# Two layers of a streaming encoder on one core: expert weights in wider pieces, the first expert's rows picked in two fp32r parts, tiles moved in SBUF, empty slots not gathered

## What is computed

```python
def moe_ffn(x, w_r, wg, wu, wd):
    xt = x.reshape(-1, D)
    logits = jnp.dot(xt, w_r, preferred_element_type=F32)
    top_v, top_i = lax.top_k(logits, TOP_K)
    w = jax.nn.softmax(top_v, axis=-1)
    gates = jnp.einsum('tk,tke->te', w, jax.nn.one_hot(top_i, N_EXPERTS, dtype=F32))
    y = jnp.zeros(xt.shape, F32)
    for e in range(N_EXPERTS):
        h = jax.nn.silu(xt @ wg[e]) * (xt @ wu[e])
        y = y + gates[:, e:e + 1] * jnp.dot(h, wd[e], preferred_element_type=F32)
    return y.astype(x.dtype).reshape(B, L, D)
```

## Time and profile before

| | us |
|---|---|
| median of 3 runs | 1627.2 (1627.18 to 1627.65) |
| profiled execution, own time | 1622.71 |
| its span, first to last instruction | 1620.9 |
| TensorE busy in the span | 1566.9 (97%) |
| VectorE / ScalarE / GpSimd busy | 1236.4 / 1000.6 / 224.7 |
| mean granted TensorE clock | 0.985 |

### The profile page before, as it was taken

The page is one execution under the profiler, slowest core; times in us unless marked ns, Lnnn a source line. Parts: engine busy times, 40 slices in busy tenths (PEclk is TensorE's granted clock), DMA queues, the critical chain, the costliest instruction groups (busy, mean ns, idle before and its releaser), DMA issues.

```text
span 1620.9 us, 21665 instructions
## 1 busy us (share of the span) xinstructions
PE 1566.9 (97%) x8425; PEld 1346.0 (83%) x8425; DVE 1236.4 (76%) x1243; ACT 1000.6 (62%) x1077; POOL 224.7 (14%) x271
## 2 busy tenths in 40 slices
PE   7989999999998999999999999999999999999996
PEld 5978899999997887888888888888888888888885
DVE  4866666664476655988888888888888888888884
ACT  4554533333455445777777777777777777777774
POOL 4703220000150223202002002002002002002000
PEclk8999999999999997999999999999999999999998
DMA  6432554444433257999999999999999999999992
GB/s 176 131 102 81 106 167 142 141 161 143 137 114 113 92 111 274 347 385 361 384 371 359 381 370 355 386 378 357 383 372 359 382 371 354 387 373 353 388 359 79
DMA packets 222517, 437.03 MB, mean 270 GB/s; under 512 B 11829, under 2 KB 65921, under 8 KB 222417
## 3 DMA queue, kind: packets, MB, share of 16 engines
q1 hardware_dynamic: 214196, 420.40, 73.6%
q0 software_dynamic: 5968, 11.84, 2.7%
q10 hardware_dynamic: 2252, 3.41, 0.7%
HBM read 428.04 MB, written 13.34 MB: 272 GB/s over the span
## 4 chain that ended last, share of the span: by engine, by line
PE 86%; DVE 6%; ACT 4%; DMA 2%; issue 1%; POOL 1%; ACTq 0%; POOLq 0%; DVEq 0%
PE bank L1856 25%; PE bank L2305 13%; PE bank L2304 13%; PE bank L2309 13%; PE bank L2318 6%; PE bank L2324 6%; PE bank L2315 6%; DVE cut_lo L1250 2%; ACT cut_hi L855 2%; PE bank L2333 2%; PE bank L1859 1%; DMA ring<-ffn_w_up 1%; ACT pe L954 1%; DMA ring<-w_in 1%; POOL acc L654 1%
## 5 line engine op out<-in xcount | busy, mean ns | idle before, releaser
L1686 DVE TENSOR_TENSOR split_lo<-raw,split_hi 128x2048 fp32r<-128x2048 f32 x336 | 768.1, 2290 | 120.0 <-ACT split_hi L1121 119.4
L1121 ACT CAST split_hi<-raw 128x2048 fp32r<-128x2048 f32 x336 | 640.1, 1909 | 245.7 <-PE bank L2309 158.5
L2304 PE MATMUL bank<-split_hi,xgT_hi 128*128 128x512 f32 x896 | 357.3, 399 | 0.0
L2305 PE MATMUL bank<-split_hi,xgT_lo 128*128 128x512 f32 x896 | 355.8, 397 | 0.0
L1250 DVE TENSOR_TENSOR cut_lo<-ring,cut_hi 128x1024 fp32r<-128x1024 f32 x124 | 154.3, 1245 | 138.8 <-ACT cut_hi L855 138.6
L1856 PE MATMUL bank<-xT_hi,cut_hi 128*128 128x320 f32 x752 | 241.5, 321 | 5.0 <-DVE xT_lo L1264 2.3
L2309 PE MATMUL bank<-split_lo,xgT_hi 128*128 128x512 f32 x896 | 245.1, 395 | 0.0
L855 ACT CAST cut_hi<-ring 128x1024 fp32r<-128x1024 f32 x124 | 129.6, 1048 | 176.8 <-PE bank L1856 170.8
L1856 PE MATMUL bank<-xT_lo,cut_hi 128*128 128x320 f32 x752 | 235.8, 314 | 0.0
L1856 PE MATMUL bank<-xT_hi,cut_lo 128*128 128x320 f32 x752 | 234.4, 312 | 0.0
L2309 PEld LDWEIGHTS bank<-split_lo,xgT_hi 128*128 128x128 f32 x896 | 168.3, 188 | 41.0
(11 more groups left out here) (283 smaller groups left out, 1615.4 us busy)
## 6 DMA issues: line engine op xcount, KB each, us to landing
raw<-moe_w_gate SPq DMA_DIRECT2D x112, 1024.0 KB, 8.2
raw<-moe_w_up SPq DMA_DIRECT2D x112, 1024.0 KB, 8.2
raw<-moe_w_down SPq DMA_DIRECT2D x112, 1024.0 KB, 6.3
ring<-w_in SPq DMA_DIRECT2D x15, 1024.0 KB, 5.5
ring<-ffn_w_gate SPq DMA_DIRECT2D x11, 1024.0 KB, 5.6
ring<-ffn_w_up SPq DMA_DIRECT2D x11, 1024.0 KB, 5.3
ring<-ffn_w_down SPq DMA_DIRECT2D x10, 1024.0 KB, 5.1
ring<-w_out SPq DMA_DIRECT2D x8, 1024.0 KB, 5.0
```

What stands on the lines that cost most here:

```text
L1121: return nc.scalar.copy(split_hi[:, i % SR, :], raw_piece(i)).then_inc(hi_ready, 1)
L1686: V.tensor_tensor(split_lo[:, i % SR, :], raw_piece(i), split_hi[:, i % SR, :].bitcast(F32), ALU.subtract).then_inc(lo_ready, 1)
L2304: TE.matmul(o, xgT_hi[:, kk, :], hi[:, c], start=kk == 0, stop=False)
L2305: TE.matmul(o, xgT_lo[:, kk, :], hi[:, c], start=False, stop=False)
```

## The change

It does the following.
- Pieces: column tiles are taken in pairs. A gate (or up) piece holds 256 rows of two neighbouring tiles (1024 columns), four gate pieces and then four up pieces per pair; the seventh tile stays as it was. In a piece, each stationary operand is used for both tiles before the next. Silu and the products of a pair are made together.
- w_down's rows are assigned to partitions so that four neighbouring rows lie in one partition; to match, the transposes of hm take every fourth column.
- The first expert's rows: x gets a high part xr_hi (a second copy by ScalarE from PSUM) and a low part xr_lo (GpSimd, six subtractions), and the pick multiplies both with Gown in fp32r.
- Gathers skip slots without a token (index out of bounds), so xg is set to zero once.
- Tiles: `empty` is gone, Gown lies behind hs, two paddings (below_xg, below_hmT_lo) are added. By the allocation order, front and loop tiles up to split_lo move 384 bytes down, xg, xgT and hs 1728 bytes down, hmT_lo 1344 bytes up. x, raw and the constants stay.
- The square of the rows goes to hs instead of xhat, one copy is moved ahead of it, and the wait for k_out ahead of four copies.

```diff
-HT_AT = [4 * _j + 11 for _j in range(FC - 1)] + [4 * FC + 7]
+WIDE = FC // 2
+GROUPS = [(8 * _g, 4, (2 * _g, 2 * _g + 1)) for _g in range(WIDE)] + [(8 * WIDE, 2, (FC - 1,))]
+HT_AT = [_a + 2 * _n + 5 + _i for _a, _n, _ms in GROUPS[:-1] for _i in range(2)] + [4 * FC + 7]
+SILU_AT = {_a + _n - 1 + SR: (_a + _n, _ms) for _a, _n, _ms in GROUPS}
+GATED_AT = {_a + 2 * _n - 1 + SR: (_a + 2 * _n, _ms) for _a, _n, _ms in GROUPS}
+
+def gate_up(q):
+    a, n, ms = GROUPS[min(q // 8, WIDE)]
+    up, s = divmod(q - a, n)
+    return up, s, ms
...
-        empty = sb("empty", [P, MAXB * NE * 4])
...
+        xr_hi = sb("xr_hi", [P, NT, D], FR, token_rows)
...
-        Gown = sb("Gown", [P, NT, P])
...
+        sb("below_xg", [P, 48])
         xg = sb("xg", [P, D])
...
         hs = sb("hs", [P, 2, 512])
+        Gown = sb("Gown", [P, NT, P], FR)
+        sb("below_hmT_lo", [P, 384])
+        token_rows = ExitStack()
+        xr_lo = sb("xr_lo", [P, NT, D], FR, token_rows)
...
-            wd_v = A["moe_w_down"][0].rearrange("e (c b p) n -> e c p b n", b=4, p=P)
+            wd_v = A["moe_w_down"][0].rearrange("e (c p b) n -> e c p b n", b=4, p=P)
...
-                        w = wg_v if j % 2 == 0 else wu_v
-                        src = w[bass.ds(e + h, 1), :, 4 * half:4 * half + 4, 512 * (j // 2):512 * (j // 2) + 512]
+                        up, s, ms = gate_up(q)
+                        n = 4 // len(ms)
+                        src = (wu_v if up else wg_v)[bass.ds(e + h, 1), :, n * s:n * s + n, 512 * ms[0]:512 * (ms[-1] + 1)]
...
-            pool.dma_start(table.rearrange("(p n) c -> p (n c)", p=P), empty[:]).then_inc(table_zero, 16)
+            pool.dma_start(table.rearrange("(p n) c -> p (n c)", p=P), A["const"][:, CONST_W:CONST_W + MAXB * NE * 4]).then_inc(table_zero, 16)
...
+            R, job = norm_end(3, KB - 1)
+            pool.wait_ge(R.full, R.filled(job))
+            for half in range(2):
+                c = slice(512 * half, 512 * half + 512)
+                for t, (t0, rows) in enumerate(TILES):
+                    R = (RS, RC)[half]
+                    pool.wait_ge(R.free, R.emptied(("xk", t, half)))
+                    nc.gpsimd.tensor_tensor(xr_lo[0:rows, t, c], x[0:rows, t, c], xr_hi[0:rows, t, c].bitcast(F32), ALU.subtract).then_inc(xr_lo_ready, 1)
+            nc.gpsimd.memset(xg[:], 0.0).then_inc(pool_zero, 1)
             for t, (t0, rows) in enumerate(TILES):
                 pool.wait_ge(rows_sq, t + 1)
                 rsqrt(rs_slot(1, "end", t), rows, D, 1)
...
+                pool.indirect_dma_start(out=xg[:], out_offset=None, in_=hx[:, :], in_offset=bass.IndirectOffsetOnAxis(ap=idc[:, 0:1], axis=0),
+                                        bounds_check=T - 1, oob_is_err=False).then_inc(xg_in, 16)
...
-                nc.scalar.copy(x[0:rows, t, 512 * half:512 * half + 512], R.bank(("xk", t, half))[0:rows, :]).then_inc(R.free, 1)
+                c = slice(512 * half, 512 * half + 512)
+                nc.scalar.copy(x[0:rows, t, c], R.bank(("xk", t, half))[0:rows, :])
+                nc.scalar.copy(xr_hi[0:rows, t, c], R.bank(("xk", t, half))[0:rows, :]).then_inc(R.free, 1)
...
+                        if k % 4 == 0:
+                            pe.wait_ge(xr_lo_ready, NT * (k // 4) + t + 1)
+                        mm(o, xr_hi[0:rows, t, P * k:P * k + P], Gown[0:rows, t, :], t == 0, False)
+                        last = mm(o, xr_lo[0:rows, t, P * k:P * k + P], Gown[0:rows, t, :], False, t == NT - 1)
...
+                        n, w = 4 // len(ms), 512 * len(ms)
+                        outs = [banks[2 * up + (FC * h + m) % 2][:] for m in ms]
+                        for k in range(n):
+                            kk = n * s + k
+                            for c, o in enumerate(outs):
+                                TE.matmul(o, xgT_hi[:, kk, :], hi[:, w * k + 512 * c:w * k + 512 * c + 512], start=kk == 0, stop=False)
+                            for c, o in enumerate(outs):
+                                TE.matmul(o, xgT_lo[:, kk, :], hi[:, w * k + 512 * c:w * k + 512 * c + 512], start=False, stop=False)
...
-                            last = TE.transpose(tb[n % 2][:, 128 * k:128 * k + 128], hm[:, m % 2, 128 * k:128 * k + 128], ident)
+                            last = TE.transpose(tb[n % 2][:, 128 * k:128 * k + 128], hm[:, m % 2, k:512:4], ident)
```

More of the change, by code:

```diff
@@ L1149, in _ @@
             act.wait_ge(RC.free, RC.emptied(("wo", 1, WO_RING.rindex("C"))))
[L1150 removed]
             x_copy(RC, 0, 1)
             x_copy(RC, 1, 1)
+            x_copy(RC, 2, 1)
             row_squares(0)
[L1154 removed]
             row_squares(1)
@@ L1200, in experts @@
                         y_copy(ip, h - 1)
-                    if q % 4 == 0 and 1 <= q // 4 <= FC:
-                        j = q // 4 - 1
-                        m = FC * h + j
-                        act.wait_ge(piece_used, ip * (2 * NP) + (NP * h + 4 * j + 2 + SR))
-                        act.wait_ge(u_free, ip * (2 * FC) + max(m, 1))
-                        if j == 0:
+                    if q in SILU_AT:
+                        used, ms = SILU_AT[q]
+                        act.wait_ge(piece_used, ip * (2 * NP) + (NP * h + used + SR))
+                        if ms[0] == 0:
                             act.wait_ge(now_ready, ip * 2 + (h + 1))
-                        nc.scalar.activation(hs[:, m % 2, :], banks[m % 2][:], ACT.Silu, scale=now_w[:, h % 2, 0:1]).then_inc(g_free, 1)
+                        for j in ms:
+                            m = FC * h + j
+                            act.wait_ge(u_free, ip * (2 * FC) + max(m, 1))
+                            nc.scalar.activation(hs[:, m % 2, :], banks[m % 2][:], ACT.Silu, scale=now_w[:, h % 2, 0:1]).then_inc(g_free, 1)
                     if q in HT_AT:
@@ L2277, in experts @@
                         for t, (t0, rows) in enumerate(TILES):
-                            last = mm(b[:, 0:2], Gown[0:rows, t, :], own[0:rows, t, :], t == 0, t == NT - 1)
+                            last = mm(b[:, 0:2], Gown[0:rows, t, :].bitcast(F32), own[0:rows, t, :], t == 0, t == NT - 1)
                         last.then_inc(RD.full, 1)
@@ L2299, in experts @@
                     if j < 2 * FC:
-                        o = banks[2 * (j % 2) + (FC * h + j // 2) % 2][:]
-                        for k in range(4):
-                            kk = 4 * half + k
-                            c = slice(512 * k, 512 * k + 512)
-                            TE.matmul(o, xgT_hi[:, kk, :], hi[:, c], start=kk == 0, stop=False)
-                            TE.matmul(o, xgT_lo[:, kk, :], hi[:, c], start=False, stop=False)
+                        n, w = 4 // len(ms), 512 * len(ms)
[6 more added lines that the diff above has]
+                                TE.matmul(o, xgT_lo[:, kk, :], hi[:, w * k + 512 * c:w * k + 512 * c + 512], start=False, stop=False)
                         pe.wait_ge(lo_ready, ip * (2 * NP) + (i + 1 + PR))
-                        for k in range(4):
-                            kk = 4 * half + k
-                            last = TE.matmul(o, xgT_hi[:, kk, :], lo[:, 512 * k:512 * k + 512], start=False, stop=kk == KB - 1)
+                        for k in range(n):
+                            kk = n * s + k
+                            for c, o in enumerate(outs):
+                                last = TE.matmul(o, xgT_hi[:, kk, :], lo[:, w * k + 512 * c:w * k + 512 * c + 512], start=False, stop=kk == KB - 1)
                     else:
@@ L2353, in _constants @@
 def _constants():
-    c = np.zeros((P, CONST_W), np.float32)
+    c = np.zeros((P, CONST_W + MAXB * NE * 4), np.float32)
     def at(name):
```

44 lines of the change are left out of this document (24 added, 20 removed).

## The result

The changed kernel takes 1604.8 us (median, 1603.5 to 1607.7) against 1627.2: a ratio of 0.9866, 95% interval 0.9849 to 0.9883. The forecast was 1626.0 with a range from 1617 to 1645, so both missed. The profiled execution took 1603.5 us, 19.2 less than that of before; its span is 19.4 us shorter.

What follows compares the result with a forecast made beforehand. TensorE was taken to pace the expert stage. Stage start +2.7 (4.4 - 1.7) and order of matmuls -3.9 gave -1.2 us: 1621.5 profiled, 1626.0 as a median, range 1617 to 1645.

Steps and rivals of the forecast that it cites:

- the moved bytes: Tiles at new SBUF addresses: taken at 0, since gate, up and down pieces differ by under 1%.
- rival 4: Matmul pitch of 0.233 us: bytes move it 0.002 either way, 8 us, 1618 or 1634; chance 0.06.
- The prediction's own sign of being wrong: TensorE's pitch changes for matmuls whose order didn't, or a stall appears inside the expert stage.
- Order of matmuls: Wide gate and up pieces: each falls from 2.80 to 2.78 us, 3.9 us less in all.
- rival 3: Gate and up pieces stay at 2.80; the 0.02 us come from hmT and banks; 1629.9, chance 0.12.
- Wider transfers: Weight pieces with longer DMA runs: worth nothing, hidden by a queue seven pieces deep.
- Pair order: Vector work ahead of a pair's first transposes: 4.95 us plus some 0.2 hidden under 5.60 on TensorE.
- Strided transposes: 224 transposes of hm loading every fourth column: taken at 0, bounded above by 18.0 us.
- rival 2: Strided stationary read of hm is slower; at double length of the load 1644.0; chance 0.18.
- The pick: First expert's rows by 48 fp32r matmuls: 1.7 us less, bounds 0 and 5.1 less.
- Contention: Ahead of the pick: GpSimd's subtractions hold up VectorE, the pick begins 4.4 us later; bounds 0.6 and 4.4.
- The end of the half clock: Left 3.2 us into the pieces, costing 1.6 us as now; bounds 1.6 less and 1.6 more.

Runs made afterwards that it cites:

- e1: The kernel before with every tile of the expert stage and front at the bytes of after, nothing else changed; 1601.8 us, ratio 0.9839.
- e2: The kernel after with its tiles back at the bytes of before, all other edits kept; 1630.7 us, ratio 1.0016.
- e12: The kernel after with w_down's old row order and the transposes of hm without a step; 1605.3 us, ratio 0.9874.
- e9: The kernel before with one padding of 192 bytes ahead of xg; 1604.8 us, ratio 0.9874.
- e10: The kernel before with one padding of 448 bytes ahead of xg; 1603.3 us, ratio 0.9868.
- e3: The kernel before with all tiles from tri_bf on 384 bytes lower, their distances kept; 1624.7 us, ratio 0.9979.
- e8: The kernel before with 64 bytes of padding ahead of hmT_lo alone; 1626.7 us.
- e5: The kernel before with one padding of 64 bytes ahead of xg; 1627.0 us.
- e7: The kernel before with 64 bytes ahead of hmT_hi and 64 more ahead of xg; 1628.1 us.
- e11: The kernel before with one padding of 320 bytes ahead of xg; 1626.4 us, ratio 1.0005.

## Why the prediction failed

**The step that failed** is the last of its parts, which takes the moved bytes at 0, and with it rival 4, which had the mechanism's name and a chance of 0.06. The runs showed 26 us in its place (e1, ratio 0.9839): 21.6 in the expert stage, by the new distances between stationary and moving tiles, and some 3 in the layers (24 to 29 in all by e1's interval). The prediction's ground was that gate, up and down pieces read at different addresses and differ by under 1%. But 0.7% of a stage of 972 us is 7 us, twice what the prediction itself called measurable. The difference of 0.02 us was the clue, not the excuse: two thirds of a down piece's matmuls read hmT_hi, which stood at distance 0 from the split tiles, all others at 64. Nor was the question put to the pace itself: 0.233 us for 512 columns is 0.020 above 512 / 2.4, and the rival gave 0.002 us of that to the bytes, without a source, where it was 0.0066 for gate and up pieces. With 24.4 in the place of 8 us the rival's good half would have read 1602. The prediction's own sign of being wrong, a changed pitch of matmuls whose order didn't change, is what the trace showed: down pieces went from 2.78 to 2.72.

**Order of matmuls, forecast -3.9.** Wrong, by rival 3's reason in another form: the 0.02 us belonged to a tile. e2 has the new order at 2.800 us per gate piece, and the gaps between expert matmuls sum to 908.2 us in after and 908.3 in e1, which has the old one.

**Wider transfers, 0.** Right (e2: no faster; SyncE's waits and landing as before).

**Pair order, hidden.** Nearly: 0.7 us in all, among them one gap in the first expert in which the transposes came 0.2 to 0.3 us late.

**Strided transposes, 0, bound 18.0.** 1.7 us: of the three distances between the starts of a group's four transposes the first stays at 0.110 us and the other two are 0.119 and 0.122 instead of 0.109, and the next matmul comes 0.007 later than in e12. The Trainium skill (SBUF — State Buffer, Door 1: The DMA port swizzle, the note on cachelines) has the direction right; the size is about a tenth of a load, not another whole one, and rival 2 is out.

**The pick, -1.7.** Right: 13.31 against 14.96 us. Records follow each other by 0.21 to 0.22 us at the half clock (621.22, 621.44, 621.65), by 0.35 where the rows change between 128 and 64 (621.65, 622.00), and by 0.27 right behind such a change (620.95, 621.22). The logits of after show the load with almost no stream beside it: with 8 moving columns, loads of 128 columns follow each other by 0.112 us before the clock falls and by 0.213 behind it. So the load's 0.213 us held, and the Trainium skill's figure that knows no clock (TensorE: Matmul & The Clock Gate, LDWEIGHTS), by which 5.1 us would have gone, doesn't hold here at 1.2 GHz.

**Contention, +4.4.** The mechanism is right, its size depends on the execution: 3.8 us in e2 and e12, 1.2 in the profiled execution of after, with ScalarE's copies in both. For the start of the stage +2.7 was forecast; with a late fall it is 3.8 - 1.65 = 2.2.

**The end of the half clock** was left as it was, rightly: 634.3 to 637.5 us has clock 0.50 in after too.

**The sum.** All of the change but the bytes was forecast at -1.2 us and measured, at the old bytes, at +2.6 (0.7 to 4.7 by e2's interval). The order's 3.9 and the 2.5 of the gaps with transposes (1.7 for the step, 0.7 for the pair order) are that miss and more; a smaller contention gives some back. The range ended at 1617, and only a case in which the bytes matter for all 4032 matmuls reaches under it.

## What to carry to other kernels

Before any tuning of a TensorE-paced loop, work out each matmul's pace from starts, compare it with its columns over the clock, and if the rest is more than it is elsewhere, look at the bytes: here a padding that puts every stationary tile of the expert stage at a multiple of 256 bytes from its moving tile was worth 21 us, alone and in one line (e9, e10). Measure it anew for another width: at 320 columns other distances were better. When a change moves tiles, the moved bytes are a part of it with a price of its own; run the old code at the new bytes before you credit the code. And a contention forecast from one trace has to ask what else, such as the clock, shifts the chain it sits in.

## What the runs showed of the hardware

The pace of 512-column fp32r matmuls with 128-column loads at the full granted clock hangs on the distance of the two operands in SBUF modulo 256 bytes. In gate and up pieces, whose twelve matmuls all have one distance, it is 0.2267 us at 0, 0.2289 at 192, 0.2331 to 0.2333 at 32, 64, 128 and 224. Moving both tiles alike (e3, 384 bytes) changes nothing. Where distances are mixed, in down pieces, the price isn't the sum of the matmuls' own: a third of them at 64 costs 0.058 of 0.080 us. The rhythm isn't set by the distance alone: at 64 it is 0.231 and 0.236 in turn in before and e3, but an even 0.233 in e8; at 128 it is 0.237 and 0.229 (e5, e7, e11). At the half granted clock no price shows: behind the first gap the first matmuls of the stage follow each other by 0.427 us, which is 512 columns at 1.2 GHz, in before (distance 64) as in e10 (distance 0). At 320 columns the layers' bytes matter as well (0.1460 against 0.1469 to 0.1478 us), but by which distance isn't known. Why all this is so stays open: no run here looks below the pace itself.
